# Second layer's up projection: normalised rows of 256 columns and weights placed by turns in its last eight chunks, last norm's vectors loaded late

## The reference

```python
D_MODEL, D_FF_2, SEQ, N_META = 1024, 4096, 256, 16
DEEPNORM_ALPHA = 4 ** 0.25
for layer in range(2):
    mix = _even_mixer(h, ...) if layer == 0 else _retention(h, ...)
    h = _layer_norm(DEEPNORM_ALPHA * h + mix, ln_g[layer, 0], ln_b[layer, 0])
    ff = jnp.square(jax.nn.relu(h @ ffn_w1[layer])) @ ffn_w2[layer]
    h = _layer_norm(DEEPNORM_ALPHA * h + ff, ln_g[layer, 1], ln_b[layer, 1])
return h[:, N_META:, :]
```

## Time and profile before

| | us |
|---|---|
| median of 3 runs | 1096.2 |
| lowest and highest of them | 1095.54, 1096.66 |
| the profiled execution, its own time | 1096.92 |
| its span, first to last instruction | 1095.1 |
| PE busy in the span | 1074.8 (98%) |
| DVE busy | 784.3 (72%) |
| ACT busy | 615.4 (56%) |
| POOL busy | 347.9 (32%) |
| granted TensorE clock, mean | 0.997 |

### The profile page before, as it was taken

One profiled execution on the slowest core, in us unless ns is written; L12 is line 12 of the kernel. 1 busy time (PEld: TensorE's weight loads), 2 busy tenths in 40 slices (PEclk: granted clock), 3 DMA queues, 4 the chain that ended last, 5 costly groups with the idle time before them and its releaser, 6 DMA issues.

```text
span 1095.1 us, 21644 instructions
## 1 busy us (share of the span) xinstructions
PE 1074.8 (98%) x8589; PEld 1028.8 (94%) x8589; DVE 784.3 (72%) x1399; ACT 615.4 (56%) x1180; POOL 347.9 (32%) x383
## 2 busy tenths in 40 slices
PE   9999999999989999999999999999999999999997
PEld 8977999999989999899999999999989999999886
DVE  5877589887579777868788544795566566998356
ACT  5657566556446657766565443674336555666432
POOL 3102423334302402145666111300033343876000
PEclk9999999999999999999999999999999999999999
DMA  8463447774656723225555565655414657555552
GB/s 239 130 198 118 118 126 210 197 194 153 211 183 200 220 82 117 78 78 192 168 180 163 180 196 167 230 174 185 154 40 143 205 166 219 192 187 172 199 193 97
DMA packets 195063, 182.10 MB, mean 166 GB/s; under 512 B 6896, under 2 KB 184467, under 8 KB 194835
## 3 DMA queue, kind: packets, MB, share of 16 engines
q1 hardware_dynamic: 193987, 175.74, 51.3%
q0 software_dynamic: 976, 4.99, 1.4%
HBM read 177.33 MB, written 1.05 MB: 163 GB/s over the span
## 4 chain that ended last, share of the span: by engine, by line
PE 88%; DVE 5%; ACT 3%; DMA 2%; issue 1%; POOL 0%; SPq 0%; DVEq 0%; ACTq 0%; POOLq 0%
PE ps L2052 24%; PE ps L2053 23%; PE ps L2054 23%; DVE wlo L1385 3%; PE ps L2665 2%; PE ps L2664 2%; PE ps L2663 2%; DMA raw<-ffn_w 1%; PE ps L2497 1%; PE ps L2229 1%; ACT whi L839 1%; PE ps L2630 1%; PE ps L2608 1%; PE ps L2480 1%; PE ps L2264 1%
## 5 line engine op out<-in xcount | busy, mean ns | idle before, releaser
L1385 DVE TENSOR_TENSOR wlo<-raw,whi 128x1024 fp32r<-128x1024 f32 x316 | 395.8, 1289 | 164.1 <-ACT whi L839 163.0
L839 ACT ACTIVATE whi<-raw 128x1024 fp32r<-128x1024 f32 x315 | 317.5, 1051 | 178.0 <-PE ps L2054 116.5
L2052 PE MATMUL ps<-xh,whi 128*128 128x256 f32 (+1 forms) x880 | 248.0, 282 | 0.5 <-DVE wlo L1385 0.4
L2053 PE MATMUL ps<-xl,whi 128*128 128x256 f32 (+1 forms) x880 | 245.5, 279 | 0.0
L2054 PE MATMUL ps<-xh,wlo 128*128 128x256 f32 (+1 forms) x880 | 245.4, 279 | 0.0
L2052 PE MATMUL ps<-xrh,whi 128*128 128x274 f32 (+2 forms) x832 | 240.7, 289 | 1.2 <-DVE wlo L1385 1.2
L2054 PE MATMUL ps<-xrh,wlo 128*128 128x274 f32 (+2 forms) x832 | 237.6, 286 | 0.0
L2053 PE MATMUL ps<-xrl,whi 128*128 128x274 f32 (+2 forms) x832 | 237.6, 286 | 0.0
L2052 PEld LDWEIGHTS ps<-xh,whi 128*128 128x128 f32 x880 | 165.8, 188 | 1.8 <-DVE wlo L1385 0.8
L2053 PEld LDWEIGHTS ps<-xl,whi 128*128 128x128 f32 x880 | 165.8, 188 | 0.1
L2054 PEld LDWEIGHTS ps<-xh,wlo 128*128 128x128 f32 x880 | 165.8, 188 | 0.0
(11 more groups left out here) (388 smaller groups left out, 2066.3 us busy)
## 6 DMA issues: line engine op xcount, KB each, us to landing
raw<-ffn_w SPq DMA_DIRECT2D x128, 512.0 KB, 4.6
raw<-ret_w_in SPq DMA_DIRECT2D x48, 512.0 KB, 4.5
raw<-even_w_in SPq DMA_DIRECT2D x24, 512.0 KB, 4.8
raw<-w_ffn_gate SPq DMA_DIRECT2D x22, 512.0 KB, 4.0
raw<-w_ffn_up SPq DMA_DIRECT2D x22, 512.0 KB, 5.3
raw<-w_ffn_down SPq DMA_DIRECT2D x16, 512.0 KB, 4.5
raw<-ret_w_out SPq DMA_DIRECT2D x16, 512.0 KB, 4.1
raw<-w_in SPq DMA_DIRECT2D x11, 512.0 KB, 5.3
```

Of the source, the lines that this page charges most:

```text
L839: A(w_half(whi, 2 * use + slot, s), raw_half(raw, 2 * use + slot, s), ACT.Copy).then_inc(w_hi_ready, 1)
L1385: V.tensor_tensor(w_half(wlo, c, s), raw_half(raw, c, s), f32(w_half(whi, c, s)), ALU.subtract).then_inc(w_lo_ready, 1)
L2052: T.matmul(dst, w[0], x[0], start=first, stop=False)
L2053: T.matmul(dst, w[0], x[1], start=False, stop=False)
```

## The change

Chunks 0 to 7 of `ffn_up1` stay on raw rows. Chunks 8 to 15 multiply the normalised rows `x1h`/`x1l` with 256 columns, with their weights placed by turns, and ACT's ReLU reads their PSUM tiles directly. For that, `layer_apply` runs for two tiles in each of the turns 0 to 3 and for none in turns 4 to 7; ACT writes `x1h` beside `h` (a second activation per tile), and POOL writes `x1l` (one subtraction per tile, at the end of its turns 0 to 3). PE waits ahead of chunk 8 for `raw_out` of chunk 7, and in chunk 8 for each tile's `x1l`. `ffn_down1` waits for `relu_ready` in place of `raw_out`. POOL loads `gains` when chunk 11 of `ffn_down1` is done.

```diff
--- before.py
+++ after.py
@@ -156,7 +156,8 @@
 
 BY_TURNS = {c for name, n in (("qkv_in", 2), ("conv_in", 4), ("mix_out", 4), ("gate_up", 22), ("down", 12), ("ple_gate", 4), ("ret_g", 8),
                               ("ret_out", 8)) for c in range(C0[name], C0[name] + n)}
-BEGINS = {c: at0 for name, first, n, at0 in (("ret_qk", 0, 4, 32), ("ret_v", 0, 8, 48), ("ffn_up1", 0, 16, 32))
+BY_TURNS.update(C0["ffn_up1"] + j for j in range(8, 16))
+BEGINS = {c: at0 for name, first, n, at0 in (("ret_qk", 0, 4, 32), ("ret_v", 0, 8, 48), ("ffn_up1", 0, 8, 32))
           for c in range(C0[name] + first, C0[name] + first + n)}
 BEGINS.update({C0["ffn_down1"] + j: 48 for j in range(16)})
 
@@ -435,7 +436,7 @@
         TILES.update({S_LN + j: (4 + j) * KD for j in range(4)})
 
 
-        X_A, X_QKV, X_FFN, X_PLE, X_B, X_LN0, X_LN1, X_RET, X_LN2 = 0, 8, 13, 21, 29, 37, 45, 53, 61
+        X_A, X_QKV, X_FFN, X_PLE, X_B, X_LN0, X_LN1, X_RET, X_LN2, X_NORM = 0, 8, 13, 21, 29, 37, 45, 53, 61, 69
 
         SUMMED = {n: KD - 2 if n in (S_X, S_MIX, S_FFN, S_LN + 3) else KD for n in range(S_LN + 4)}
         ACC0 = {n: sum(SUMMED[m] for m in range(n)) for n in SUMMED}
@@ -766,7 +767,7 @@
                 nc.gpsimd.tensor_tensor(xol[:, hd, :], oa[:, hd, :], f32(xoh[:, hd, :]), ALU.subtract).then_inc(oa_lo, 1)
             forget_low(1)
 
-            def hidden(base, cols, hi, lo):
+            def hidden(base, cols, hi, lo, rows=None):
 
                 def low(m, slot):
                     pool.wait_ge(f_hi, base + m + 1)
@@ -781,6 +782,10 @@
                         if u % 2 == 1 and not (is_first(i) and u == 1):
                             for back in (3, 2):
                                 low(m - back, (u - back) % 4)
+                    if rows is not None and i < 4:
+                        for k in (2 * i, 2 * i + 1):
+                            pool.wait_ge(xh_ready, rows + k + 1)
+                            nc.gpsimd.tensor_tensor(x1l[:, k, :], h[:, k, LAST], f32(x1h[:, k, :]), ALU.subtract).then_inc(x_ready, 1)
 
                 repeat(pool, FT2 // 4, turn)
                 for m in (FT2 - 2, FT2 - 1):
@@ -817,9 +822,10 @@
 
             repeat(pool, 4, y_low)
             sums(S_LN + 2, y, LAST)
+            hidden(FT + FT2, LAST, f1h, f1l, X_NORM)
+            pool.wait_ge(mm_done, E0["ffn_down1"] + 12)
             for n, name in enumerate(("ln_g_2", "ln_b_2")):
                 pool.dma_start(gains[:, n, :], a[name][1, 1:2, :].broadcast_to([P, D])).then_inc(const_in, 16)
-            hidden(FT + FT2, LAST, f1h, f1l)
 
 
         @block.scalar
@@ -902,7 +908,7 @@
                 act.wait_ge(norm_ready, KD * j + k + 1)
                 A(h[:, at(k), cols], y[:, at(k), cols], ACT.Identity, bias=b, scale=g).then_inc(hn_ready, 1)
                 if dst is not None:
-                    A(dst[:, at(k), cols], y[:, at(k), cols], ACT.Identity, bias=b, scale=g).then_inc(xh_ready, 1)
+                    A(dst[:, k, 0:size(cols)], y[:, at(k), cols], ACT.Identity, bias=b, scale=g).then_inc(xh_ready, 1)
 
             def raw_columns(j):
 
@@ -1277,12 +1283,20 @@
                             split_in(name, i, 2, u)
                         for m in range(2):
                             t = 4 * i + 2 * u + m
+                            if j and i >= 4:
+                                act.wait_ge(mm_done, E0[name] + 2 * i + u + 1)
+                                A(ra[:, 2 * u + m, cols], ps[2 * ((P0[name] + u) % 2) + m][:, 0:N1], ACT.Relu).then_inc(relu_ready, 1)
+                                continue
                             act.wait_ge(raw_ready, base - FT + (16 if j else 0) + t + 1)
                             A(ra[:, 2 * u + m, cols], rw[:, 2 * u + m, cols], ACT.Relu, bias=b_col[:, 2 * u + m:2 * u + m + 1]).then_inc(relu_ready, 1)
                         if not (is_first(i) and u == 0):
                             for m in range(2):
                                 high(4 * i + 2 * u + m - 2, 2 - 2 * u + m)
-                    layer_apply(j, i, cols)
+                    if j == 0:
+                        layer_apply(j, i, cols)
+                    elif i < 4:
+                        for k in (2 * i, 2 * i + 1):
+                            layer_apply(j, k, cols, x1h)
 
                 def high(t, slot):
                     act.wait_ge(f_mul, base + t + 1)
@@ -1893,12 +1907,19 @@
                             split_at(C0[name] + 2, (0,))
                             layer_var(j, cols)
                         t = 4 * i + 2 * u
+                        if j and i >= 4:
+                            split_in(name, i, 2, u)
+                            continue
                         raw_tiles(E0[name] + 2 * i + u + 1, 2 * ((P0[name] + u) % 2), 2 * u, S_LN + j, raw0 + t, (relu_ready, base + t - 2), cols)
                         if start:
                             split_at(C0[name] + 2, (1,))
                         else:
                             split_in(name, i, 2, u)
-                    layer_apply(S_LN + j, j, i, cols)
+                    if j == 0:
+                        layer_apply(S_LN + j, j, i, cols)
+                    elif i < 4:
+                        for k in (2 * i, 2 * i + 1):
+                            layer_apply(S_LN + j, j, k, cols)
 
                 repeat(dve, 8, turn)
 
@@ -2552,8 +2573,15 @@
 
             def up(j, layer, x0, raw0, cols):
 
-                outputs(f"ffn_up{layer}", FT2 // 4, raw(cols), rows_r, x_from(x0), raw_out,
+                outputs(f"ffn_up{layer}", 4 if layer else 8, raw(cols), rows_r, x_from(x0), raw_out,
                         lambda t: raw0 + t + 1 if not isinstance(t, int) or t >= 0 else 0, beside=lambda: stat(S_LN + j, cols))
+                if layer:
+                    pe.wait_ge(raw_out, raw0 + 8)
+                    for t in range(8, 16):
+                        if t >= 10:
+                            pe.wait_ge(relu_ready, FT2 + 2 * t - 2)
+                        product(C0["ffn_up1"] + t, t % 2, pair("ffn_up1", t, N1), rows_x1, TOK1, 256,
+                                ready=x_from(X_NORM) if t == 8 else None).then_inc(mm_done, 1)
 
             def mlp(j, layer, x0, raw0, hidden0, cols, f, at_f):
 
@@ -2667,7 +2695,7 @@
 
             for j in range(14):
                 if j % 8 == 0:
-                    pe.wait_ge(raw_out, FT2 // 2 + 8 + FT2 // 2 - 1 + j // 8)
+                    pe.wait_ge(relu_ready, 2 * FT2 - 2 + 2 * (j // 8))
                 for k in range(4):
                     if k % 2 == 0:
                         pe.wait_ge(w_lo_ready, 2 * (C0["ffn_down1"] + j) + 1 + k // 2)
```

## The result

| | before | after |
|---|---|---|
| median | 1096.08 (4 runs) | 1104.89 (4 runs, 1102.72 to 1106.09) |
| ratio after/before | | 1.0078, 95% interval 1.0066 to 1.0089 |
| profiled execution, its own time | 1096.92 | 1106.09 |
| its span | 1095.1 | 1104.0 |
| mean granted clock, all runs after | 0.997 (profiled) | 0.992 to 0.995 |

The change makes the kernel slower by 0.78%. The forecast was 1102.9 with a range of 1097 to 1107.

What follows compares the result with a forecast made beforehand. PE, busy for 98%, was taken as the bound, with DVE nearly full and becoming the bound in turns 0 to 3. Terms -2.05, -1.2 +0.3, +1.35, +3.8 and +4.5 gave +6.7 us on 1096.2: 1102.9, range 1097 to 1107.

Steps and rivals of the forecast that it cites:

- A: Chunks 8 to 15 of ffn_up1: 256-column matmuls with weights by turns save PE 5.4 ns each, -2.05 us.
- B: Moving the vectors' load: PE's wait at chunk 3 goes, -1.2 us; delay in ffn_down1's last two chunks, +0.3.
- C: DVE's turns 0 to 3: a second layer_apply lengthens turns to 12.9 us; PE waits 1.35 us for chunk 6.
- D: Step to chunk 8: PE waits 3.8 us for raw_out of chunk 7, which DVE begins late.
- E: Within chunk 8: PE waits 4.5 us for tiles 6 and 7, normalised at the end of DVE's turn 3.
- Rival 2: Chunk 8: the waits there take PE's clock down, adding 1.25 to 2.5 us, 1104.2 to 1105.4; chance 0.22.
- Rival 1: DVE's turns 0 to 3: DVE keeps up despite the second layer_apply, time not longer, 1095.7 us; chance 0.16.
- Rival 3: End of ffn_down1: the vectors' load delays the last two chunks by the full +2 us, 1104.6; chance 0.07.
- Rival 4: Chunks 8 to 15: columns and placement do not set the 118.7 ns spacing, so nothing is saved, 1105.0; chance 0.05.

Runs made afterwards that it cites:

- two_tiles: Kernel before, with only DVE's and ACT's layer_apply done for two tiles in each of turns 0 to 3, products on raw rows: 1101.22 us, ratio 1.0035.
- raw_turns: Kernel before, with the weights of chunks 8 to 15 of ffn_up1 placed by turns, rows still raw with 258 columns: 1096.32 us, ratio 1.0000.
- load_late: Kernel before, with only the last norm's vectors loaded later, after chunk 11 of ffn_down1: 1095.93 us, ratio 0.9991; again 1096.06, 0.9989.
- filler: bank_wait plus 48 matmuls into a bank nobody reads, just ahead of PE's wait for tile 6 in chunk 8: 1103.58 us, ratio 1.0059.
- bank_wait: Changed kernel, but chunk 8 waits for raw_out of chunk 6 and chunk 9 for that of chunk 7: 1105.22 us, ratio 1.0070.
- switch_12: Changed kernel with normalised rows from chunk 12, tiles spread over turns 0 to 5, banks waited for as in bank_wait: 1099.39 us, ratio 1.0019.
- the second measurement: The changed kernel itself, unaltered, measured again against the kernel before: 1104.94 us, ratio 1.0067.
- norm_no_turns: Changed kernel with the weights of all 16 chunks of ffn_up1 placed as before, not by turns: 1105.83 us, ratio 1.0082.

## Why the prediction was right

**A, -2.05.** Measured 8 x (5.71 - 5.44) = -2.1. The size is right. But I bought both edits as one form from `ret_out` and could not say which mattered; the answer is neither alone. The rule in the Trainium skill ("TensorE: Matmul & The Clock Gate", Back-to-back issue gap), 0.8 ns for two columns, is near what the columns bring at the old placement (about 1 ns) and has no term for the placement. The section gives this rule for an isolated matmul and says that a stream of weight loads and matmuls is spaced otherwise, which my prediction left out. The traces agree with that: the rule makes 109.2 ns of 256 columns, and the two measured spacings are 117.8 and 113.3.

**B, -1.2 + 0.3.** Measured -1.2 in the stage. At the end the changed kernel's traces show nothing, PE's load waits 0.2 us before and after; of the ten traces with the late load three are 0.25 to 0.45 us longer there. So the +0.3 is the price in some executions and not the usual one. Neither of the two other early-load traces, two_tiles and raw_turns, has the wait at chunk 3, so the -1.2 holds for the execution that I read, and by the ratios of load_late for the median.

**C, 12.9 us per turn and a wait of 1.35.** By its own schedule the prediction's wait is 1.25 (942.2 - 940.95), and D's 3.7; the slips of 0.1 change nothing. DVE's turn is 12.9, made of the parts I had: 3.0 us for two tiles (1.6 + 1.3 forecast) and contention at the next `raw_tiles`. In place of the latter the trace has a pause of 0.5 us in which DVE waits for ACT's `whi`, since ACT has three activations ahead of it. I had put those at nothing. The two errors cancel.

The base was luck too. I took 11.1 us as DVE's own need and 0.1 to 0.35 us as its margin, but with the late load alone the same turn takes 9.8 us of DVE's time (load_late). The second tile brought DVE back to where it meets POOL: the second split of a turn lasts 3.32 us again. The wait is 1.09 us, 1.26 from start to start.

**D, 3.8.** Measured 3.26 of idle time.

**E, 4.5: the term that was mis-sized.** The idle time in chunk 8 is 2.07 us for tile 6 and 0.3 for tile 7. Tile 6 came 8.1 us after PE resumed (7.8 forecast), but PE was slow: tiles 0 to 5 took 5.8 us and not 4.1, because the clock was at 0.50 from 960.1 to 963.6. Chunk 8 with its waits lasts 11.1 us from its first matmul, against 9.9 forecast, and chunk 9 another 0.4 over 5.44. The slow tiles 0 to 5 cost nothing by themselves, since PE waited for tile 6 behind them; the slow stretch behind tile 6 does.

**Rival 2, the clock.** It came true, in both traces of the changed kernel, and the mean clock of 0.994 or 0.995 in its other runs fits it (two spells of 3.4 us at half make 0.003 of the span). I gave it 0.22 although two waits of 3.8 us were forecast beside a row that showed the fall after a wait of 3.8 us. That was the mistake: by my own rows it belonged to the likeliest case. Its price was 1.25 to 2.5; filler puts it at 1.1 in the changed kernel, since a part of the slow time is spent where PE would wait anyway, and at 2.0 in bank_wait, where none is.

**The sum.** Stage: +6.4 forecast without the clock; with the clock kept up, filler shows +6.1. With it the changed kernel shows +7.2. Another 0.3 us lies outside the span: own time less span is 2.1 us in the kernels built on the changed one (2.5 in switch_12) and 1.8 in those built on the one before. I did not foresee it and did not find its cause. 7.2 + 0.3 = 7.5 agrees with the ratio of the second measurement (1.0067, 7.3 us) and with the lower end of the first one's interval (7.2 us); the 8.8 us between the first medians hold about 1 us that no trace explains. One source is possible and not shown: the +7.2 is counted from an execution with the wait at chunk 3, and from raw_turns's stage of 92.50, without it, it is 8.2. That 1104.89 lies inside the range rests on its width: the clock's 1.1 us was priced in a rival with a chance of 0.22.

**Rivals 1, 3 and 4.** DVE did not keep up, nor could it: two_tiles shows the loss with nothing else changed. The vectors' load never cost 2 us at the end, at most 0.45. The spacing fell as forecast.

## What to carry to other kernels

Where a late step of one stage feeds the next products, look at where in the list of the loaded engine the last input is made: moving two tiles ahead of two other items gave back 5.9 us, about 2 of them by way of the clock, and taking away the wait in front of them gave nothing. Price a second wait that stands behind the first as one event that ends when the last input arrives. When a forecast contains a wait as long as one after which the trace shows the clock at half, put the slow clock into the likeliest case.

## What the hardware showed that I had not expected

- The spacing of matmuls depends on rows and placement together: 118.7, 119.4, 117.8 and 113.3 ns in the four combinations. What in the placement does it was not tried, nor whether the two columns count or where the rows lie.
- DVE and POOL can be locked into slowing each other: the same work per turn keeps DVE busy for 9.8 us or for 11.35, according to how the two run against each other. In the two traces with 11.35 us ACT had waited 3.3 and 4.7 us for the weights of chunk 3, in load_late's two 0.8 us or less; PE had waited in only one of them.
- Work that nobody reads can pay: 48 matmuls in a wait of 5.7 us kept the clock at 1.00 and took 2.0 us off chunks 8 and 9.
- After the two waits of the changed kernel the clock was at 0.50, at 1.00 and at 0.50 again within 10.3 us, each slow spell lasting 3.4 us. With nearly the same waits (3.2 and 2.0 us) norm_no_turns's trace has only the first spell, so the length of a wait alone does not settle it.
